# Loading each round of weights with two DMAs of 1 MB into two buffers, in place of four of 512 KB into four

## What is computed

```python
D_MODEL = 2048
DEPTH = 2
D_FF = -(-_FF_RAW // 256) * 256        # 5632
...
def _mix_out(x, o_swa, o_ret, g_r, w_o):
    ...
    return x + jnp.einsum('btc,cd->btd', cat, w_o)

def _ffn(x, g, w_gate_up, w_down):
    xn = _rmsnorm(x, g)
    a, b = jnp.split(jnp.einsum('btd,df->btf', xn, w_gate_up), 2, axis=-1)
    return x + jnp.einsum('btf,fd->btd', jax.nn.silu(a) * b, w_down)
```

## Time and profile before

| what | us |
|---|---|
| median of 3 runs | 2620.09 |
| lowest, highest run | 2619.52, 2621.95 |
| profiled execution, its time | 2618.75 |
| profiled execution, span of the core | 2617.2 |
| TensorE (PE) busy | 2587.1 |
| VectorE (DVE) busy | 1486.0 |
| ScalarE (ACT) busy | 1251.2 |

### The profile page before, as it was taken

The page is one execution under the profiler, slowest core; times in us unless marked ns, Lnnn a source line. Parts: engine busy times, 40 slices in busy tenths (PEclk is TensorE's granted clock), DMA queues, the critical chain, the costliest instruction groups (busy, mean ns, idle before and its releaser), DMA issues.

```text
span 2617.2 us, 53415 instructions
## 1 busy us (share of the span) xinstructions
PE 2587.1 (99%) x19706; PEld 2558.3 (98%) x19706; DVE 1486.0 (57%) x2405; ACT 1251.2 (48%) x2227; POOL 160.8 (6%) x235
## 2 busy tenths in 40 slices
PE   8999999999999999999999999999999999999997
PEld 8999999999999999999999999999999999999997
DVE  6566665555555555555455666665555555554555
ACT  6455555444444444444444555554444444444443
POOL 2211102000000000000020110120000000000000
PEclk9999999999999999999999999999999999999998
DMA  7666655555555555555564666555555555555554
GB/s 243 203 203 202 201 180 182 169 167 164 165 166 163 166 159 168 167 166 161 165 215 149 203 206 196 188 181 168 165 165 164 160 168 164 165 161 163 165 168 141
DMA packets 131389, 458.97 MB, mean 175 GB/s; under 512 B 16357, under 2 KB 18685, under 8 KB 131328
## 3 DMA queue, kind: packets, MB, share of 16 engines
q1 hardware_dynamic: 113328, 404.05, 49.8%
q0 software_dynamic: 14880, 48.39, 6.0%
q10 hardware_dynamic: 3120, 5.71, 0.6%
HBM read 436.18 MB, written 27.54 MB: 177 GB/s over the span
## 4 chain that ended last, share of the span: by engine, by line
PE 64%; issue 32%; DVE 2%; ACT 1%; POOLq 1%; DVEq 0%; DMA 0%; ACTq 0%; SPq 0%
PE ps L1052 20%; PE ps L1054 20%; PE ps L1056 20%; PE ps L1218 1%; PE ps L1277 1%; PE ps L1286 1%; DVE rot_tmp L959 0%; PE ps L1239 0%; DVE w_lo L685 0%; PE ps L1268 0%; POOLq L1361 0%; POOLq L1363 0%; DVE x_res L1030 0%; DVE rstd L705 0%; ACT w_hi L373 0%
## 5 line engine op out<-in xcount | busy, mean ns | idle before, releaser
L685 DVE TENSOR_TENSOR w_lo<-raw,w_hi 128x512 fp32r<-128x512 f32 x1572 | 1057.3, 679 | 874.7 <-ACT w_hi L373 855.2
L373 ACT ACTIVATE w_hi<-raw 128x512 fp32r<-128x512 f32 x1572 | 965.2, 621 | 1106.6 <-PE ps L1056 1101.4
L1052 PE MATMUL ps<-xg_hi,w_hi 128*128 128x288 f32 x4224 | 1264.3, 299 | 12.7 <-DVE w_lo L685 12.4
L1056 PE MATMUL ps<-xg_hi,w_lo 128*128 128x288 f32 x4224 | 1247.3, 295 | 0.0
L1054 PE MATMUL ps<-xg_lo,w_hi 128*128 128x288 f32 x4224 | 1245.4, 295 | 0.0
L1052 PEld LDWEIGHTS ps<-xg_hi,w_hi 128*128 128x128 f32 x4224 | 794.7, 188 | 21.4 <-issue 10.7
L1054 PEld LDWEIGHTS ps<-xg_lo,w_hi 128*128 128x128 f32 x4224 | 793.9, 188 | 0.6
L1056 PEld LDWEIGHTS ps<-xg_hi,w_lo 128*128 128x128 f32 x4224 | 794.3, 188 | 0.0
L1054 PE MATMUL ps<-cat_lo,w_hi 128*128 128x288 f32 x1024 | 303.4, 296 | 0.0
L1056 PE MATMUL ps<-cat_hi,w_lo 128*128 128x288 f32 x1024 | 302.2, 295 | 0.0
L1052 PE MATMUL ps<-cat_hi,w_hi 128*128 128x288 f32 x1024 | 300.8, 294 | 0.0
(11 more groups left out here) (200 smaller groups left out, 1188.4 us busy)
## 6 DMA issues: line engine op xcount, KB each, us to landing
raw<-w_gate_up SPq DMA_DIRECT2D x352, 512.0 KB, 3.6
raw<-w_in SPq DMA_DIRECT2D x178, 512.0 KB, 3.7
raw<-w_down SPq DMA_DIRECT2D x160, 512.0 KB, 3.6
raw<-w_o SPq DMA_DIRECT2D x64, 512.0 KB, 4.0
st<-state POOLq DMA_DIRECT2D x16, 1024.0 KB, 10.1
new_rs<-st POOLq DMA_DIRECT2D x16, 1024.0 KB, 7.5
raw<-w_down SPq DMA_DIRECT2D x32, 256.0 KB, 2.6
yT<-x_res ACTq DMA_DIRECT2D x4, 576.0 KB, 3.1
```

Source lines behind the costliest of these rows:

```text
L373: nc.scalar.activation(w_hi[q][:, 0:n, :], raw[s][:, n * (j % 2):n * (j % 2) + n, :], ACT.Copy).then_inc(hi_ready[q], 1)
L685: nc.vector.tensor_tensor(w_lo[q][:, 0:n, :], raw[s][:, n * (j % 2):n * (j % 2) + n, :], w_hi[q][:, 0:n, :].bitcast(F32), ALU.subtract).th ...
L1052: nc.tensor.matmul(out, w_hi[q][:, t, cols], x_hi[:, x, :], start=(k == 0), stop=False, skip_group_check=True)
L1056: ins = nc.tensor.matmul(out, w_lo[q][:, t, cols], x_hi[:, x, :], start=False, stop=(k == kts - 1), skip_group_check=True)
```

## The change

Two `raw` buffers of 1 MB stand in place of four of 512 KB; the space is the same. A half of a round (two pieces, 1 MB in one run of HBM) is one DMA, with 8 KB for each partition in two pieces of 4 KB. It feeds four steps. SP issues it when DVE has done the last of the four steps of the same half in the round before (`split_ready[3]`). ACT waits for the half's semaphore, and ACT and DVE index the larger buffer. In the third `w_down` round the second half is one DMA of 512 KB in place of two of 256 KB.

```diff
-        raw = [sb(f"raw{s}", [P, 4, PAIR]) for s in range(4)]
+        raw = [sb(f"raw{s}", [P, 8, PAIR]) for s in range(2)]
...
-        raw_loaded = [sem(f"raw_loaded{s}") for s in range(4)]
+        raw_loaded = [sem(f"raw_loaded{s}") for s in range(2)]
...
-            def load_round(r, w, layer, n, kt0=0, sizes=FULL, chunks=4):
-                kt = kt0
-                for s in range(chunks):
-
-                    j = 2 * s + 1
-                    sp.wait_ge(split_ready[j % 4], 2 * r + j // 4 + 1)
-                    block, t = kt // 4, kt % 4
-                    src = w[bass.ds(layer, 1), bass.ds(n, 1), block:block + 1, :, t:t + sizes[s], :]
-                    sp.dma_start(raw[s][:, 0:sizes[s], :],
-                                 src.rearrange("l n b p t c -> p (l n b t) c")).then_inc(raw_loaded[s], 16)
-                    kt += sizes[s]
+            def load_round(r, w, layer, n, kt0=0, sizes=FULL, halves=2):
+                block = kt0 // 4
+                for h in range(halves):
+
+                    sp.wait_ge(split_ready[3], 2 * r + h + 1)
+                    blocks = (sizes[2 * h] + sizes[2 * h + 1]) // 4
+                    src = w[bass.ds(layer, 1), bass.ds(n, 1), block:block + blocks]
+                    sp.dma_start(raw[h][:, 0:4 * blocks, :].rearrange("p (b t) c -> p b (t c)", t=4),
+                                 src.rearrange("l n b p t c -> p (l n b) (t c)")).then_inc(raw_loaded[h], 16)
+                    block += blocks
...
-            load_round(DEPTH * ROUNDS, w_in, 0, 0, chunks=2)
+            load_round(DEPTH * ROUNDS, w_in, 0, 0, halves=1)
...
-                    act.wait_ge(raw_loaded[s], r * 16 + 16)
+                    act.wait_ge(raw_loaded[j // 4], r * 16 + 16)
...
-                    nc.scalar.activation(w_hi[q][:, 0:n, :], raw[s][:, n * (j % 2):n * (j % 2) + n, :],
+                    nc.scalar.activation(w_hi[q][:, 0:n, :], raw[j // 4][:, n * (j % 4):n * (j % 4) + n, :],
...
-                    nc.vector.tensor_tensor(w_lo[q][:, 0:n, :], raw[s][:, n * (j % 2):n * (j % 2) + n, :],
+                    nc.vector.tensor_tensor(w_lo[q][:, 0:n, :], raw[j // 4][:, n * (j % 4):n * (j % 4) + n, :],
```

## The result

| | before | after |
|---|---|---|
| median, us | 2620.43 (7 runs, 2619.52 to 2621.95) | 2629.64 (7 runs, 2628.24 to 2632.45) |
| profiled execution, its time, us | 2618.75 | 2628.35 |
| its span, us | 2617.2 | 2626.8 |

The ratio is 1.0037, 95% interval 1.0026 to 1.0047: the change made the kernel 9.2 us slower. The time lies inside the predicted range, but the likeliest case, within 0.2%, did not come; the first rival did, a little beyond its upper end (+9.2 against +9.1).

What follows compares the result with a forecast made beforehand. PE's back-to-back matmuls were taken as the bound, with loads having time to spare. Terms 2.1 + 0.6 + 0.5 = 3.2 us on the profiled 2618.75 gave 2621.95, by the median 2623.3; range 2620.6 to 2631.

Steps and rivals of the forecast that it cites:

- the likeliest case: Whole kernel: time within 0.2% (5.2 us) of before, chance 0.66; the forecast of +1 to +5.2 us had 0.54 of it.
- the first rival: Whole kernel slower because start and contended loads come near their upper ends: +5.3 to +9.1 us, chance 0.16.
- What a steady round needs: Steady rounds: a 1 MB load takes 5.0 us against 6.2 us at the tightest w_down place, PE waits 0 us.
- The dear-load rival: At 16 w_down column blocks, 1 MB taking 7.2 us misses the slack by 1.0 us each: at least 2639, chance 0.15.
- The start: First load: 1 MB lands at 9.4 us, PE begins 2.7 us later and recovers 0.6: net 2.1 us.
- the pauses: First round: two pauses of PE, 0.28 us each, swallowed by the later start, recovering 0.6 us.
- The bias copy: Load issued at 36.6 us beside GpSimd's copy: PE 0.4 to 1.6 us late, taken as 0.6.
- The states: First attention group's state loads, both layers: weight load delayed beside them, 0 to 4.0 us, taken as 0.5.
- The sum: Whole kernel: start, bias copy and states, 2.1 + 0.6 + 0.5 = 3.2 us, ends +1.0 and +9.1.
- the prediction's own signs: Profile after: 1 MB landings 4.8 to 5.6 us, PE's first wait 10.9, `w_lo` waits beyond the start growing about 1 us at most.

Runs made afterwards that it cites:

- e2: Kernel before, with both 512 KB loads of a half issued only once step 3 of that half is split; 2620.66 us, ratio 1.0001.
- e3: Kernel before with its early issues, but ScalarE starts a half only when both its 512 KB loads have landed; 2622.71 us, ratio 1.0008.
- e8: Kernel before, both 512 KB loads of a half issued at the later point and ScalarE waiting for both; 2640.84 us, ratio 1.0075.
- e4: Changed kernel, with GpSimd's copy of the bias rows held until step 0 of the fourth round is split; 2627.02 us, ratio 1.0023.
- e7: Changed kernel, with the first half of every round issued one step later; 2659.52 us, ratio 1.0152.
- e5: Changed kernel, with the last attention group's state loads in each layer made to wait for a ScalarE split; 2628.98 us, ratio 1.0033.
- e9: Changed kernel, first round in four loads, bias copy later, every group's state loads released by the VectorE step that releases the weight load; 2621.21 us, ratio 1.0004.
- e1: Changed kernel, with the first round loaded in four 512 KB pieces, each with its own semaphore; 2628.64 us, ratio 1.0031.
- e10: Kernel before, with the bias copy later and every attention group's state loads released by the VectorE step that releases the weight load; 2620.0 us, ratio 0.9998.
- e6: Changed kernel, with the first round in four loads, the bias copy later and the last groups' state loads later; 2624.03 us, ratio 1.0013.

## Why the prediction came out low

**What a steady round needs, 0 us: right.** The 1 MB load was taken at 5.0 us and lands in 4.9. At the `w_down` blocks, with 6.2 us of slack, PE never waits; ScalarE's 66.2 us for gate/up weights stay inside the ring, as worked out there: 48 waits of 1.4 us on average, where it had waited 0.9 us for PE at 46 of them before, so 0.5 us more each, the forecast size. The dear-load rival fell. The Trainium skill, "DMA: Bandwidth & Descriptors", section "Rules for kernel authors", asks to issue early and wait late. Here e2 and e3 show each half of that rule given up for 0.3 and 2.3 us, and e8 and the change show the cost of giving up both, 21.1 and 9.2 us.

**The start, 2.1 us: nearly right, in part by luck.** The first load landed at 1.78 + 8.98 = 10.76 us, the upper end of 10.8 rather than the middle of 9.4, and PE's first wait was 12.28, not 10.9. PE also recovered more, 1.9 us by 25 us and not 0.6: the pauses gave 0.9, and 1.0 came from a term that the prediction did not have. PE's first matmuls follow every 0.24 us, before for 5.4 us from its start and after for 3.3 us, and then every 0.13, so nine fewer of them were slow (the profile's granted clock reads 1.00 in both stretches, so it does not show why they are slow). Two errors of opposite sign made a net of 2.18 us at 25 us, 2.53 from 39 us on. In the profiled executions of e4 and e7, with the same 1 MB start, PE's first wait was 12.25 and 12.26 us, in that of e5 14.81.

**The bias copy, 0.6 us: mis-sized, 2.67 measured.** The step said "7.3 + 1.2 = 8.5, or 7.3 + 2.4 = 9.7" for the 1 MB, from the one chunk issued at 36.6 us. The load issued at 39.48 took 10.5. The later chunks beside the same copy were the nearer measure: in the trace of before those issued at 37.8 and 40.3 took 9.1 and 10.3 us.

**The states, 0.5 us: mis-sized and misplaced, 3.6 measured.** This is the largest error. The step looked at the first attention group alone, where layer 0 costs nothing and layer 1 0.91. It left out the last group of each layer, 1.28 and 1.39. The trace of before had shown the sign: SP's line of loads there, the issue at 309.96, the chunk behind the one at 308.11 above:

```profile
DMA to landing us min/median/max: 8.8/8.8/8.8
```

Before, that chunk cost nothing: it is chunk 0 of the next round, issued two steps earlier than the change issues that half, and PE wants it only at 324.26, 5.5 us after its landing. The slack of the attention groups, 7.35 us, held against that 8.8, and not only the slack of gate/up and `w_down`, would have shown the risk. The sentence that the 1 MB "stands in the queue two steps earlier than the second chunk did, ahead of the state loads" was the failing step: in the last groups it stands 0.64 and 0.68 us behind. It failed in the first groups as well. GpSimd's state load in layer 0 came at 81.54, as early as before (81.50), while PE and with it the weight load were already 5.2 us late, so the 1 MB, issued at 86.06, stood 4.5 us behind it and took 9.2 us. That this cost nothing is luck: VectorE had the first step split at 96.6 and PE took it at 96.79.

**The sum.** 3.2 us were forecast. Of the measured 9.8 in the profiled executions 2.5 + 2.7 + 3.6 = 8.8 are these three terms, and 1.0 is a pace of the matmuls that has nothing to do with the loads. The first rival had the right mechanism, and its top, +9.1, is where the medians landed; it deserved more than 0.16. That the time lies inside the range is owed to this rival being taken into it; the forecast itself ended at +5.2. Of the prediction's own signs, the landings (4.9 to 5.2 us) and PE's first wait (12.28) came as said, but PE's waits for `w_lo` grew by 9.9 - 4.1 = 5.8 us beyond the start, where about 1 was allowed.

## What to carry to other kernels

A larger load into fewer buffers spends slack twice, by the later issue and by the later first use; work out the slack that is left in every stage, not only in the longest one, and hold it against the slowest loads of the trace, not the median. Where another queue's bulk transfer is issued beside a load on the path, look at which of the two is issued first: here under half a microsecond decided nearly 3 us of landing. That order can be set with one wait on the other queue, as e9 does.

## What the runs showed of the hardware that was not expected

**Which transfer is ahead.** A 1 MB weight load issued up to 0.38 us behind a GpSimd state load still passes with 5.6 to 6.7 us, one from 0.54 us on takes 8.2 or more; GpSimd's own issue takes 0.89 us. The Trainium skill, "Trainium Kernel Development and Optimization", section "Key Constraints", says that transfers from the queues of several engines share the same DMA engines and interleave. The traces agree that they share them, and show more than an even interleaving: which transfer's bytes start first decides what the weight load takes. The DMA view of the changed kernel has it (queue, packets, MB, share of the DMA engines); q1 carries SP's loads, q0 those of GpSimd. From 178.6 to 181.5 us, with the weight load 0.28 us behind the state load's issue, only weights move:

```profile
q1 hardware_dynamic: 209, 0.86, 95.7%
```

From 314.1 to 315.1, with 0.64 us, only the state moves:

```profile
q0 software_dynamic: 37, 0.15, 74.1%
```

In the packet records of the thirty loads of the table's first four rows, a weight load that starts first has its first packet 1.0 to 1.1 us after its issue, a state load that starts first 1.6 us after its own. Up to 0.51 us the weights started first in all 23 cases, from 0.54 us on the state in all seven, and the difference of these two times, some 0.6 us, is about the lag that decides. The state loads lost nothing by coming second: from the second group on they took 7.5 to 8.8 us in e9, 8.0 to 8.8 in the changed kernel.

**The clock after a wait.** A wait of PE of 2.77 us at 50.0 in e1 was followed by three microseconds at a granted clock of 0.50 (1.2 GHz), one of 2.90 us at 51.4 in the changed kernel's profiled execution by none. In e5, e7 and e8 the waits at the same place, 2.26, 2.89 and 2.92 us, had 0.50 behind or around their end too, so the changed kernel's profiled execution is the exception. The window of the changed kernel behind its wait:

```profile
52.00:54.00 2.00, 2.00 (x17) 2.00 (x16) 1.92 (x4) 1.14 (x4) 2.00 (x5) 1.00 0.08 16
```

It shows 1.00 (2.4 GHz). So nearly the same wait can cost over a microsecond more in one execution than in the next (in e1 PE's delay against the kernel before grew by 1.5 us between 50 and 65 us). That may be part of the scatter of the changed kernel's runs; no run shows it.

**Two paces.** In `w_down` the same matmuls, with no wait and a clock of 1.00, run in one of two paces in an execution. PE's timeline, the same two matmuls before, and then after:

```profile
2340.13 0.29 PE L1052 MATMUL ps<-hid_hi,w_hi 128*128 128x288 f32 x1
...
2580.11 0.29 PE L1052 MATMUL ps<-hid_hi,w_hi 128*128 128x288 f32 x1
```

```profile
2349.01 0.30 PE L1051 MATMUL ps<-hid_hi,w_hi 128*128 128x288 f32 x1
...
2590.01 0.30 PE L1051 MATMUL ps<-hid_hi,w_hi 128*128 128x288 f32 x1
```

239.98 us against 241.00, 0.4%. Both kernels with four buffers and those with two are found on either side: e10, e1 and e6 took 239.98 there, e2, e3, e4, e5 and e9 241.00 (e7 and e8, with small waits of PE in that stretch, 240.6 and 240.4). The same happens in layer 0, 179.69 or 180.44 us for another such stretch. Its cause stays open; it moves a run by up to 2 us and says that single profiled executions shouldn't be compared more closely than that.
